# Attention in a one-core encoder layer: row maxima from the higher parts alone, as two 64-row products side by side

## The chip, the cores and the metric

One NeuronCore of a Trainium2 chip. The metric is the time of one launch of the whole layer in microseconds (us), median over runs. Engines: PE multiplies matrices (PEld is its loading of weights), DVE is the vector engine, ACT the scalar engine, POOL is GpSimd, SP issues transfers.

## What is computed

One encoder layer for two sequences, 512 and 1024 tokens, with shared weights. The change lies in its attention:

```python
q = apply_axial_rope(rms_norm(q.reshape(b, l, 16, 64), q_norm), cos, sin)
k = apply_axial_rope(rms_norm(k.reshape(b, l, 4, 64), k_norm), cos, sin)
s = jnp.einsum("bqgrd,bkgd->bgrqk", q_blk, k) * 64 ** -0.5
p = jax.nn.softmax(s, axis=-1)          # 16 query heads, 4 key heads
o = jnp.einsum("bgrqk,bkgd->bqgrd", p, v)
```

Before it come an RMS norm and the input projection, beside it a state-space branch and gates, after it the merge, an output projection and an MLP. The softmax is the same whatever number near the row's maximum is subtracted from the scores.

## The kernel before

The layer is one program in four parts: `project`, `gates_and_states`, `attention`, `tail`. Each engine's order of work is written out by hand, with semaphores between engines. A float32 value is held as a higher and a lower part (type fp32r), and a product is made as hi x hi + hi x lo + lo x hi.

Attention runs from about 633 to 1081 us of the span. A *unit* is one query head and one block of 512 queries: 16 units for the short sequence (A), 32 for the long one (B). A unit goes over the tiles of 128 keys, 4 in A and 8 in B; one tile is a *step*. There are 64 + 256 = 320 steps. In each step PE issues:

- the scores of the tile, transposed (keys by queries), two products (L1954, L1955): `k1` holds the higher part of the keys twice, in partitions 0 to 63 and 64 to 127, `q1` the higher and the lower part of the queries; `k2` holds the lower part of the keys in rows 0 to 63 and ones in row 64, `q2` the higher part of the queries and, in row 64, the negated maxima. So the second product has 65 rows, and the scores come out with the maximum subtracted.
- one product for the maxima of the unit *two units ahead* (`max_part`, L1923): 128 queries as the weights against 512 keys, 128 rows, so (hi + lo) queries x hi keys. In A one such product makes a bank of which DVE takes the maximum (L1831, 128x512); in B two products fill two banks and DVE reduces both at once (128x1024), so every second step. There are 56 + 256 = 312 of these products: 14 units of A with 4 and 32 of B with 8, the first two of B during the last two units of A, two in a step. Units 0 and 1 have theirs in `first_max` (L1521), ahead of attention.
- three products for the values of the step three steps back (`output`, L1905 with 128 columns of weights, L1906 with 64, L1908 with 128); the last waits for the lower part of the probabilities.

ACT takes the exponential of each score bank (L1789) and casts it to the higher part on odd steps (L1794); DVE casts on even steps (L1874), makes one lower part in four (L1864), and the maxima; POOL makes the other three lower parts (L1743). SP loads the queries of a unit into `q1` and `q2` (`load_q`, L189 to L191) when its last scores are done, and places the maxima in `q2` (`place_max` for A, L202; `place_max_parts` for B, L197). In A the queries of a maximum are every fourth one, so its weights are read with a stride of four elements; in B they are contiguous. Lines L163 to L209 are the class `Middle` with the places; POOL sets the row of ones at L1307, at the end of `gates_and_states`, after PE is done with the block of activations that lies there. PE turns and splits the values into banks of the maxima in the first iteration (L183, `V_TURN`), and waits for the split at the first steps of heads 2 and 3.

Of the kernel before, what the change touches and what calls it, by code (L numbers as in the profile page):

```python
# [27 lines left out]
P = 128  # L28
D_MODEL = 1024
D_FF = 4096  # L30
HEAD = 64
NQ, NKV = 16, 4
LEN_A, LEN_B = 512, 1024
TOK = LEN_A + LEN_B
BLK = 512
# [14 lines left out]
def f32(ap):  # L50

    return ap.bitcast(F32)
# [73 lines left out]
class Middle:  # L126
# [39 lines left out]
                         ).then_inc(landed, 16)  # L166

    def load_low_keys(self, sp, roped, n, tok, h0, h1):
        sp.dma_start(f32(self.k2[0:HEAD, h0:h1, tok]),
                     roped[1, NQ + h0:NQ + h1, :, tok].rearrange("h d n -> d h n")).then_inc(self.k_in[n], 16)  # L170

    def load_v(self, sp, proj, n, tok):
# [13 lines left out]
    def load_q(self, sp, roped, kv, head, blk):  # L186
        tok = bass.ds(blk * BLK, BLK)
        hi, lo = roped[0][head][:, tok], roped[1][head][:, tok]
        sp.dma_start(f32(self.q1[kv][0:HEAD]), hi).then_inc(self.q_in[kv], 16)  # L189
        sp.dma_start(f32(self.q1[kv][HEAD:P]), lo).then_inc(self.q_in[kv], 16)  # L190
        sp.dma_start(f32(self.q2[kv][0:HEAD]), hi).then_inc(self.q_in[kv], 16)  # L191

    def place_max_parts(self, sp, u, s):

        for j in range(BLK // P):
            sp.wait_ge(self.max_found, 4 * u + (2 + j + 1))
            sp.dma_start(f32(self.q2[s][HEAD:HEAD + 1, j * P:(j + 1) * P]),  # L197
                         f32(self.nmax[s][:, j:j + 1])).then_inc(self.nmax_in[s], 16)

    def place_max(self, sp, u, s):  # L200
        sp.wait_ge(self.max_found, 4 * u + (2 + BLK // P))
        sp.dma_start(f32(self.q2[s][HEAD:HEAD + 1]).rearrange("o (p j) -> o p j", p=P),  # L202
                     f32(self.nmax[s][:])).then_inc(self.nmax_in[s], 16)

    def max_query(self, kv, j, near=False):

        if near:
            return self.q1[kv][:, j * P:(j + 1) * P]
        return self.q1[kv].rearrange("d (p j) -> d j p", p=P)[:, j]  # L209


class Ahead:
# [773 lines left out]
def gates_and_states(nc, block, st, sh, mid, ps, w_in, proj, mix, roped, done):  # L986
# [12 lines left out]
    with ExitStack() as ctx:  # L999
# [82 lines left out]
        def all_batches(eng, batch):  # L1082

            batch(Batch(None, 0), True, False)
            with eng.Fori(0, BATCHES // 2 - 1) as i:
                batch(Batch(i, 1), False, False)
                batch(Batch(i, 2), False, False)
            batch(Batch(None, BATCHES - 1), False, True)
# [5 lines left out]
        def _(sp):  # L1094
# [71 lines left out]
                store_gate(5)  # L1166

            all_batches(sp, batch)
            mid.place_max(sp, 0, 0)
            mid.load_q(sp, roped, 3, 12, 0)  # L1170
            mid.place_max(sp, 1, 1)
# [72 lines left out]
        def _(pool):  # L1244
# [58 lines left out]
            pool.wait_ge(whi_ready, 2)  # L1303
            pool.tensor_tensor(w_lo[1][:], w_raw[1][:], f32(w_hi[1][:]), ALU.subtract).then_inc(wlo_ready, 1)
            all_batches(pool, batch)
            pool.wait_ge(summed, BATCHES * GB - 1)
            pool.memset(f32(mid.k2[HEAD:HEAD + 1]), 1.0).then_inc(mid.ones_set, 1)  # L1307

            pool.wait_ge(evicted, BATCHES * GB + 3)
            pool.wait_ge(mid.ones_set, 1)  # L1310

        @block.vector
        def _(dve):
# [227 lines left out]
def attention(nc, block, st, mid, fore, ps, proj, roped, mix_y, mix, mix_t, w_tail):  # L1541
# [7 lines left out]
    with ExitStack() as ctx:  # L1549
# [361 lines left out]
        @block.tensor  # L1911
        def _(pe):
            pe.sem_inc(pv_done, QKP)
            def max_part(sq, u, s, kt):

                per = sq.n // 4
                j, half = divmod(kt, per)
                if half == 0:

                    pe.wait_ge(max_found, 4 * u + (j - 1 if sq is A else j + 1))  # L1920
                bank = MX_BANK + (j if sq is A else 2 * (j % 2) + half)
                key0 = (sq.kt0 + 4 * half) * P
                mm = pe.matmul(ps[:, bank], mid.max_query(s, j, sq is B),  # L1923
                               k1[:, s, key0:key0 + BLK], start=True, stop=True)
                if half == per - 1:
                    mm.then_inc(max_mm, 1)

            for n, sq in enumerate(SEQS):
                pe.wait_ge(k_in[n], (16, 32 + 16 * NKV)[n])
                pe.wait_ge(ones_set, (1, 2 + B.n)[n])  # L1930

                def iteration(it, last):
                    for kv in range(NKV):
# [11 lines left out]
                        for kt in range(sq.n):  # L1945
# [3 lines left out]
                            if sq is A and isinstance(it, int) and it == 0 and kv == 0 and kt < 2:  # L1949
# [2 lines left out]
                            out = ps[:, ST_BANK + kt % 2]  # L1952
                            keys = slice(tile * P, (tile + 1) * P)
                            pe.matmul(out, k1[:, kv, keys], q1[kv][:], start=True, stop=False)  # L1954
                            pe.matmul(out, k2[0:HEAD + 1, kv, keys], q2[kv][0:HEAD + 1], start=False,  # L1955
                                      stop=True).then_inc(scored, 1)
                            if sq is A and isinstance(it, int) and it == 0:
                                if kv == 0 and kt == LAG:

                                    pe.wait_ge(v2_ready, 1)  # L1960
                                    pe.wait_ge(ones_set, 2)
                                if kv == 1 and kt == LAG:

                                    pe.wait_ge(v2_ready, 2)
                                if kv >= 2 and kt < 2:

                                    pe.wait_ge(v2_ready, 2 * kv - 1 + kt)
                            if sq is A and isinstance(it, int) and it == 0 and kv == 0 and kt == 0:

                                pe.wait_ge(mid.y_ready, GROUPS // BATCH + 1)  # L1970
                            if sq_ahead:
                                for part in range(sq_ahead.n // sq.n):
                                    max_part(sq_ahead, ahead, s_ahead, kt * (sq_ahead.n // sq.n) + part)
                            i = v_part(V_TURN, sq, it, kv, kt)
                            if i is not None:
                                pe.wait_ge(k_in[1], 32)
# [1067 lines left out]
```

## Time and profile before

| | |
|---|---|
| median of 3 runs | 2490.22 us (2488.33 to 2495.74) |
| span of the profiled execution | 2487.5 us |
| the profiled execution's own time | one of the above; which one is not told |
| PE / PEld busy | 2467.0 / 2192.8 us |
| DVE / ACT / POOL busy | 1690.4 / 1122.7 / 1081.6 us |
| granted TensorE clock | 1.000 |

The span runs from the first to the last instruction. The busy time of PE comes from modelled ends: a product's row is longer than the distance to the next product's start. The distance between starts is what a product takes in a dense stream. The start of a PEld row is the start of a weight load.

### The profile page before, as it was taken

What the parts mean: (1) busy time and instruction counts of PE and PEld (TensorE: products, weight loads), DVE (VectorE), ACT (ScalarE), POOL (GpSimd) and SP (SyncE); (2) the same over time, 40 slices, a digit from 0 to 9 for tenths busy, and PEclk for the clock granted to TensorE, in tenths of its full rate; (3) what the DMA queues carried; (4) which work ended last, traced back from release to release, by engine and by line L of the source; (5) the groups of instructions that cost most, each with busy time, mean ns of one, the idle gap of its engine ahead of it and who ended that gap; (6) DMA issues with size and microseconds to landing.
All of it is one profiled execution on the core that took longest, in us unless ns stands there. A gap on an engine that the chain in (4) does not pass through costs nothing.

```text
span 2487.5 us, 37690 instructions
## 1 busy us (share of the span) xinstructions
PE 2467.0 (99%) x12320; PEld 2192.8 (88%) x12320; DVE 1690.4 (68%) x2352; ACT 1122.7 (45%) x1902; POOL 1081.6 (43%) x906
## 2 busy tenths in 40 slices
PE   8999999999999999999999999999999999999999
PEld 6888888888777777778888889999999999999999
DVE  7986588988888888886666786444446854444442
ACT  7554122121777777763444344333334343333341
POOL 0004765654667766754444423333333343333332
PEclk9999999999999999999999999999999999999999
DMA  5445233232653121244656643222222432222221
GB/s 186 173 155 183 83 94 93 78 94 82 157 124 84 45 66 44 45 137 145 200 206 197 215 170 129 68 69 69 68 68 81 140 136 69 68 69 69 68 69 68
DMA packets 160253, 271.29 MB, mean 109 GB/s; under 512 B 47216, under 2 KB 63088, under 8 KB 159984
## 3 DMA queue, kind: packets, MB, share of 16 engines
q1 hardware_dynamic: 159824, 269.19, 34.4%
q8 instruction: 82, 1.34, 0.2%
q14 instruction: 59, 0.48, 0.1%
q10 hardware_dynamic: 288, 0.27, 0.0%
HBM read 200.08 MB, written 59.24 MB: 104 GB/s over the span
## 4 chain that ended last, share of the span: by engine, by line
PE 96%; DVE 2%; issue 1%; POOL 1%; DMA 1%; ACT 0%; ACTq 0%; SPq 0%; DVEq 0%; POOLq 0%
PE banks L63 16%; PE banks L65 16%; PE banks L64 16%; PE banks L2907 6%; PE banks L2909 6%; PE banks L2910 6%; PE p_acc L63 3%; PE p_acc L64 3%; PE p_acc L65 3%; PE banks L1955 3%; PE banks L1954 3%; PE banks L1908 3%; PE banks L1923 3%; PE banks L1906 3%; PE banks L1905 3%; PE banks L1493 1%
## 5 line engine op out<-in xcount | busy, mean ns | idle before, releaser
L63 PE MATMUL banks<-block,t_whi 128*128 128x384 f32 (+1 forms) x1088 | 386.5, 355 | 0.8 <-DVE t_x L2752 0.5
L65 PE MATMUL banks<-block,t_wlo 128*128 128x384 f32 (+1 forms) x1088 | 385.9, 355 | 0.0
L1743 POOL TENSOR_TENSOR a_plo<-a_p,a_phi 128x512 fp32r<-128x512 f32 x236 | 305.4, 1307 | 142.9 <-DVE a_phi L1874 135.9
L2689 DVE TENSOR_TENSOR f_x<-banks,f_x 128x384 f32<-128x384 f32 x256 | 142.6, 557 | 291.1 <-PE banks L65 285.7
L64 PE MATMUL banks<-block,t_whi 128*128 128x384 f32 (+1 forms) x928 | 331.9, 358 | 0.0
L2907 PE MATMUL banks<-block,t_whi 128*128 128x384 f32 x800 | 268.0, 335 | 2.1 <-DVE block L2820 0.8
L2910 PE MATMUL banks<-block,t_wlo 128*128 128x384 f32 x800 | 267.3, 334 | 0.0
L2427 POOL TENSOR_TENSOR t_wlo<-t_wraw,t_whi 128x1024 fp32r<-128x1024 f32 x67 | 164.2, 2451 | 219.2 <-ACT t_whi L2448 219.2
L2909 PE MATMUL banks<-block,t_whi 128*128 128x384 f32 x768 | 256.6, 334 | 0.0
L2432 POOL TENSOR_TENSOR t_wlo<-a_quotient,t_whi 128x512 fp32r<-128x512 f32 x96 | 142.1, 1480 | 220.0 <-ACT t_whi L2463 220.0
L1789 ACT ACTIVATE a_p<-banks 128x512 f32<-128x512 f32 x320 | 190.7, 596 | 95.9 <-PE banks L1955 86.9
L63 PEld LDWEIGHTS banks<-block,t_whi 128*128 128x128 f32 x1088 | 204.3, 188 | 17.8 <-issue 2.0
L65 PEld LDWEIGHTS banks<-block,t_wlo 128*128 128x128 f32 x1088 | 204.2, 188 | 15.1
L2432 POOL TENSOR_TENSOR t_wlo<-f_s,t_whi 128x512 fp32r<-128x512 f32 x64 | 84.3, 1317 | 268.6 <-ACT t_whi L2463 268.6
L2432 POOL TENSOR_TENSOR t_wlo<-t_wraw,t_whi 128x512 fp32r<-128x512 f32 x96 | 130.9, 1364 | 158.0 <-ACT t_whi L2463 157.9
L1831 DVE TENSOR_REDUCE stage<-banks 128x1 fp32r<-128x1024 f32 (+1 forms) x184 | 191.9, 1049 | 2.6 <-PE banks L1923 1.9
L64 PEld LDWEIGHTS banks<-block,t_whi 128*128 128x128 f32 x928 | 174.3, 188 | 15.4 <-issue 0.5
L2448 ACT ACTIVATE t_whi<-t_wraw 128x1024 fp32r<-128x1024 f32 x71 | 75.3, 1061 | 210.2 <-PE banks L65 204.9
L63 PE MATMUL p_acc<-block,w_hi 128*128 128x512 f32 x384 | 152.0, 396 | 8.7 <-DVE block L785 8.7
L2463 ACT ACTIVATE t_whi<-f_s 128x512 fp32r<-128x512 f32 x128 | 80.5, 630 | 170.6 <-PE banks L65 138.8
L2907 PEld LDWEIGHTS banks<-block,t_whi 128*128 128x128 f32 x800 | 150.2, 188 | 3.4 <-issue 2.4
L2463 ACT ACTIVATE t_whi<-a_quotient 128x512 fp32r<-128x512 f32 x112 | 70.7, 631 | 181.8 <-PE banks L65 161.9
(329 smaller groups left out, 6343.8 us busy)
## 6 DMA issues: line engine op xcount, KB each, us to landing
t_wraw<-w_tail_t SPq DMA_DIRECT2D x136, 512.0 KB, 3.8
a_quotient<-w_tail_t SPq DMA_DIRECT2D x64, 512.0 KB, 3.8
block<-roped_scratch SPq DMA_DIRECT2D x146, 128.0 KB, 2.7
w_raw<-w_in_t SPq DMA_DIRECT2D x31, 512.0 KB, 4.0
proj_scratch<-s_gate SPq DMA_DIRECT2D x48, 256.0 KB, 2.0
t_graw<-proj_scratch SPq DMA_DIRECT2D x24, 512.0 KB, 3.9
p_sw<-p_qn SPq DMA_DIRECT2D x60, 128.0 KB, 2.1
roped_scratch<-p_r_hi SPq DMA_DIRECT2D x30, 256.0 KB, 2.2
```

Source lines behind the costliest of these rows:

```text
L63: pe.matmul(out, whi, xhi, start=start, stop=False)
L64: pe.matmul(out, whi, xlo, start=False, stop=False)
L65: return pe.matmul(out, wlo, xhi, start=False, stop=stop)
L1743: pool.tensor_tensor(p_lo[s][:], p32[s][:], f32(p_hi[s][:]), ALU.subtract).then_inc(plo_pool, 1)
L1789: act.activation(p32[kt % QKP][:], ps[:, ST_BANK + kt % 2], ACT.Exp, scale=HEAD ** -0.5).then_inc(exp_done, 1)
L1831: dve.tensor_reduce(nmax[s][:, j:j + 1], src, AX.X if sq is A else AX.XY, ALU.max, negate=True).then_inc(max_found, 1)
L2427: pool.tensor_tensor(w_lo[j % 2][:], w_raw[j % 2][:], f32(w_hi[j % 2][:]), ALU.subtract).then_inc(wlo_ready, 1)
L2432: pool.tensor_tensor(ring_lo[t % 4], source(t), f32(ring_hi[t % 4]), ALU.subtract).then_inc(lo_pool.sem, 1)
L2463: act.activation(ring_hi[t % 4], source(t), ACT.Copy).then_inc(f_hi_ready, 1)
L2907: pe.matmul(out, ring_hi[s][:, k], x_hi, start=fresh and k == 0, stop=False, skip_group_check=True)
L2909: pe.matmul(out, ring_hi[s][:, k], x_lo, start=False, stop=False, skip_group_check=True)
L2910: mm = pe.matmul(out, ring_lo[s][:, k], x_hi, start=False, stop=last, skip_group_check=True)
```

## The change

The maxima are taken from the products of the higher parts alone (64 rows). Two such products, the first with rows 0 to 63 of `q1` and `k1`, the second with rows 64 to 127 of `q2` and `k1`, are issued one behind the other (`max_pair`): in A for two banks at steps 0 and 2 of a unit, at the seam for the two halves of one maximum in each step, in B for the two halves at every even step. For this the halves of `k2` and `q2` change places: lower keys and higher queries lie in rows 64 to 127, the ones in rows 0 to 63 of `k2`, the maxima in row 0 of `q2`, zeros in rows 1 to 63. The second score product has 128 rows. POOL clears four places of 64x512 before it sets the ones (now 64 rows), `ones_set` counts four more, SP waits for the four before the first placing, and PE waits for both value splits at step 0 of heads 2 and 3.

```diff
--- before.py
+++ after.py
@@ -166,7 +166,7 @@
                          ).then_inc(landed, 16)
 
     def load_low_keys(self, sp, roped, n, tok, h0, h1):
-        sp.dma_start(f32(self.k2[0:HEAD, h0:h1, tok]),
+        sp.dma_start(f32(self.k2[HEAD:P, h0:h1, tok]),
                      roped[1, NQ + h0:NQ + h1, :, tok].rearrange("h d n -> d h n")).then_inc(self.k_in[n], 16)
 
     def load_v(self, sp, proj, n, tok):
@@ -188,25 +188,26 @@
         hi, lo = roped[0][head][:, tok], roped[1][head][:, tok]
         sp.dma_start(f32(self.q1[kv][0:HEAD]), hi).then_inc(self.q_in[kv], 16)
         sp.dma_start(f32(self.q1[kv][HEAD:P]), lo).then_inc(self.q_in[kv], 16)
-        sp.dma_start(f32(self.q2[kv][0:HEAD]), hi).then_inc(self.q_in[kv], 16)
+        sp.dma_start(f32(self.q2[kv][HEAD:P]), hi).then_inc(self.q_in[kv], 16)
 
     def place_max_parts(self, sp, u, s):
 
         for j in range(BLK // P):
             sp.wait_ge(self.max_found, 4 * u + (2 + j + 1))
-            sp.dma_start(f32(self.q2[s][HEAD:HEAD + 1, j * P:(j + 1) * P]),
+            sp.dma_start(f32(self.q2[s][0:1, j * P:(j + 1) * P]),
                          f32(self.nmax[s][:, j:j + 1])).then_inc(self.nmax_in[s], 16)
 
     def place_max(self, sp, u, s):
         sp.wait_ge(self.max_found, 4 * u + (2 + BLK // P))
-        sp.dma_start(f32(self.q2[s][HEAD:HEAD + 1]).rearrange("o (p j) -> o p j", p=P),
+        sp.dma_start(f32(self.q2[s][0:1]).rearrange("o (p j) -> o p j", p=P),
                      f32(self.nmax[s][:])).then_inc(self.nmax_in[s], 16)
 
-    def max_query(self, kv, j, near=False):
-
+    def max_query(self, kv, j, near=False, rows=slice(0, P)):
+
+        queries = self.q2[kv] if rows.start else self.q1[kv]
         if near:
-            return self.q1[kv][:, j * P:(j + 1) * P]
-        return self.q1[kv].rearrange("d (p j) -> d j p", p=P)[:, j]
+            return queries[rows, j * P:(j + 1) * P]
+        return queries[rows].rearrange("d (p j) -> d j p", p=P)[:, j]
 
 
 class Ahead:
@@ -1166,6 +1167,7 @@
                 store_gate(5)
 
             all_batches(sp, batch)
+            sp.wait_ge(mid.ones_set, NKV)
             mid.place_max(sp, 0, 0)
             mid.load_q(sp, roped, 3, 12, 0)
             mid.place_max(sp, 1, 1)
@@ -1303,11 +1305,13 @@
             pool.wait_ge(whi_ready, 2)
             pool.tensor_tensor(w_lo[1][:], w_raw[1][:], f32(w_hi[1][:]), ALU.subtract).then_inc(wlo_ready, 1)
             all_batches(pool, batch)
-            pool.wait_ge(summed, BATCHES * GB - 1)
-            pool.memset(f32(mid.k2[HEAD:HEAD + 1]), 1.0).then_inc(mid.ones_set, 1)
+            for kv in range(NKV):
+                pool.wait_ge(summed, BATCHES * GB - 2 + kv // 2)
+                pool.memset(f32(mid.q2[kv][0:HEAD]), 0.0).then_inc(mid.ones_set, 1)
+            pool.memset(f32(mid.k2[0:HEAD]), 1.0).then_inc(mid.ones_set, 1)
 
             pool.wait_ge(evicted, BATCHES * GB + 3)
-            pool.wait_ge(mid.ones_set, 1)
+            pool.wait_ge(mid.ones_set, NKV + 1)
 
         @block.vector
         def _(dve):
@@ -1911,23 +1915,25 @@
         @block.tensor
         def _(pe):
             pe.sem_inc(pv_done, QKP)
-            def max_part(sq, u, s, kt):
-
-                per = sq.n // 4
-                j, half = divmod(kt, per)
-                if half == 0:
-
-                    pe.wait_ge(max_found, 4 * u + (j - 1 if sq is A else j + 1))
-                bank = MX_BANK + (j if sq is A else 2 * (j % 2) + half)
-                key0 = (sq.kt0 + 4 * half) * P
-                mm = pe.matmul(ps[:, bank], mid.max_query(s, j, sq is B),
-                               k1[:, s, key0:key0 + BLK], start=True, stop=True)
-                if half == per - 1:
-                    mm.then_inc(max_mm, 1)
+            def max_pair(sq, u, s, kt):
+
+                for i, rows in enumerate((slice(0, HEAD), slice(HEAD, P))):
+                    j, half = (kt + i, 0) if sq is A else (kt // 2, i)
+                    if sq is A:
+                        pe.wait_ge(max_found, 4 * u + (j - 1))
+                    elif half == 0:
+
+                        pe.wait_ge(max_found, 4 * u + (j + 1))
+                    bank = MX_BANK + (j if sq is A else 2 * (j % 2) + half)
+                    key0 = (sq.kt0 + 4 * half) * P
+                    mm = pe.matmul(ps[:, bank], mid.max_query(s, j, sq is B, rows),
+                                   k1[rows, s, key0:key0 + BLK], start=True, stop=True)
+                    if sq is A or half:
+                        mm.then_inc(max_mm, 1)
 
             for n, sq in enumerate(SEQS):
                 pe.wait_ge(k_in[n], (16, 32 + 16 * NKV)[n])
-                pe.wait_ge(ones_set, (1, 2 + B.n)[n])
+                pe.wait_ge(ones_set, NKV + (1, 2 + B.n)[n])
 
                 def iteration(it, last):
                     for kv in range(NKV):
@@ -1952,25 +1958,27 @@
                             out = ps[:, ST_BANK + kt % 2]
                             keys = slice(tile * P, (tile + 1) * P)
                             pe.matmul(out, k1[:, kv, keys], q1[kv][:], start=True, stop=False)
-                            pe.matmul(out, k2[0:HEAD + 1, kv, keys], q2[kv][0:HEAD + 1], start=False,
+                            pe.matmul(out, k2[:, kv, keys], q2[kv][:], start=False,
                                       stop=True).then_inc(scored, 1)
                             if sq is A and isinstance(it, int) and it == 0:
                                 if kv == 0 and kt == LAG:
 
                                     pe.wait_ge(v2_ready, 1)
-                                    pe.wait_ge(ones_set, 2)
+                                    pe.wait_ge(ones_set, NKV + 2)
                                 if kv == 1 and kt == LAG:
 
                                     pe.wait_ge(v2_ready, 2)
-                                if kv >= 2 and kt < 2:
-
-                                    pe.wait_ge(v2_ready, 2 * kv - 1 + kt)
+                                if kv >= 2 and kt == 0:
+
+                                    pe.wait_ge(v2_ready, 2 * kv)
                             if sq is A and isinstance(it, int) and it == 0 and kv == 0 and kt == 0:
 
                                 pe.wait_ge(mid.y_ready, GROUPS // BATCH + 1)
                             if sq_ahead:
-                                for part in range(sq_ahead.n // sq.n):
-                                    max_part(sq_ahead, ahead, s_ahead, kt * (sq_ahead.n // sq.n) + part)
+                                if sq_ahead is not sq:
+                                    max_pair(sq_ahead, ahead, s_ahead, 2 * kt)
+                                elif kt % 2 == 0:
+                                    max_pair(sq_ahead, ahead, s_ahead, kt)
                             i = v_part(V_TURN, sq, it, kv, kt)
                             if i is not None:
                                 pe.wait_ge(k_in[1], 32)
```

## Rows read from the trace of the kernel before

**Rows 1.** The page: its head and the busy time of each engine.

```profile
span 2487.5 us, 37690 instructions
PE 2467.0 (99%) x12320; PEld 2192.8 (88%) x12320; DVE 1690.4 (68%) x2352; ACT 1122.7 (45%) x1902; POOL 1081.6 (43%) x906
```

**Rows 2.** Stretches; busy us (count) of PE, PEld, DVE, ACT, POOL; clock, DMA, GB/s.

```profile
640.00:730.00 90.00, 88.62 (x383) 69.75 (x383) 79.71 (x125) 71.98 (x124) 61.37 (x55) 1.00 0.56 138
730.00:1060.00 330.00, 330.00 (x1429) 256.17 (x1429) 276.12 (x330) 250.52 (x423) 232.01 (x182) 1.00 0.23 55
1060.00:1077.00 17.00, 17.00 (x73) 12.36 (x72) 15.15 (x18) 15.41 (x28) 11.35 (x8) 1.00 0.09 16
```

**Rows 3.** The chain of waits from 730 to 1060 us, by line.

```profile
by line: PE banks L1955 17.0%; PE banks L1954 16.7%; PE banks L1906 16.5%; PE banks L1908 16.5%; PE banks L1923 16.4%; PE banks L1905 16.3%; DVE a_plo L1864 0.2%; DVE stage L1831 0.2%; issue 0.2%; DVE a_phi L1874 0.1%
```

**Rows 4.** Groups of PE, 730 to 1060 us: count | busy us, mean ns | idle.

```profile
L1955 PE MATMUL banks<-block 65*128 65x512 f32 x238 | 95.4, 401 | 0.0
L1954 PE MATMUL banks<-block 128*128 128x512 f32 x238 | 94.5, 397 | 0.0
L1923 PE MATMUL banks<-block 128*128 128x512 f32 x239 | 93.0, 389 | 0.0
```

**Rows 5.** Timeline of one step: start us, us, engine, line.

```profile
861.09 0.40 PE L1954 MATMUL banks<-block 128*128 128x512 f32 x1
...
861.32 0.40 PE L1955 MATMUL banks<-block 65*128 65x512 f32 x1
861.32 0.19 PEld L1923 LDWEIGHTS banks<-block 128*128 128x128 f32 x1
861.56 0.39 PE L1923 MATMUL banks<-block 128*128 128x512 f32 x1
...
861.79 0.39 PE L1905 MATMUL banks<-a_phi,a_v 128*128 128x512 f32 x1
...
862.01 0.39 PE L1906 MATMUL banks<-a_phi,a_v 128*64 128x512 f32 x1
...
862.24 0.39 PE L1908 MATMUL banks<-a_plo,a_v 128*128 128x512 f32 x1
...
862.47 0.40 PE L1954 MATMUL banks<-block 128*128 128x512 f32 x1
```

**Rows 6.** Line 1923 (ns least/median/most), and timelines near 641 and 728 us.

```profile
L1923 PEld LDWEIGHTS banks<-block x312: 186/191/311, 633.6 to 1059.6; 128*128 128x128 f32 x156
L1923 PE MATMUL banks<-block x312: 389/389/499, 633.8 to 1059.9; 128*128 128x512 f32 x156
...
640.74 0.31 PEld L1923 LDWEIGHTS banks<-block 128*128 128x128 f32 x1
...
728.33 0.19 PEld L1923 LDWEIGHTS banks<-block 128*128 128x128 f32 x1 [0.43 <-DVE stage L1831]
728.34 0.50 PE L1923 MATMUL banks<-block 128*128 128x512 f32 x1
...
728.67 0.39 PE L1905 MATMUL banks<-a_phi,a_va 128*128 128x512 f32 x1
```

**Rows 7.** DVE's reductions, 730 to 1060 us; waits of 640 to 730, 1060 to 1077.

```profile
L1831 DVE TENSOR_REDUCE stage<-banks 128x1 fp32r<-128x1024 f32 x119 | 144.4, 1213 | 2.6 <-PE banks L1923 1.9
...
PEld banks L1923 <- DVE stage L1831: 2.3, 5, 0.6
...
POOL a_plo L1743 <- DVE a_phi L1874: 6.6, 7, 1.4
PEld banks L1908 <- POOL a_plo L1743: 1.4, 4, 0.5
```

**Rows 8.** Timeline of POOL, and the chain of waits, before attention.

```profile
618.57 5.24 POOL L1307 MEMSET block<- 1x6144 f32 x1 [25.76 <-PE banks L65]
...
625.95 7.12 DMA block<-stage
633.27 0.47 PE banks L1954
```

## The prediction

> **What bounds the kernel now.** I read the page first: the product engine is busy 99% of the span, the vector engine 68%, GpSimd 43% [rows 1]. Then the stretches: the change touches only attention, about 633 to 1081 us, so what it is worth is read there. From 730 to 1060 us the sequence of 1024 tokens is swept and PE is busy 330.00 of 330 us; DVE is busy 276.12, ACT 250.52, POOL 232.01, at a granted clock of 1.00 [rows 2]. The chain of waits says the same from the other side: over that stretch six lines of PE hold 16 to 17% each and nothing else holds over 0.2% [rows 3]. So there a product less is time less, if nothing new is put beside it. From 640 to 730 us, the sequence of 512, PE is busy 88.62 of 90 and DVE 79.71 [rows 2]: still PE, with DVE close behind.
>
> The timeline of one step shows the unit of account. A step is six products, L1954 to L1954 from 861.09 to 862.47, that is 1.38 us or 0.23 for each [rows 5]. One of the six is the maximum's (L1923). The row of a product says 0.39 us, but its successor starts 0.23 later: 0.23 is the price of a product in a dense stream, and the other 0.16 is its modelled tail, hidden under the next one. The weights of a product are loaded at the start of the product before it (the load of L1923 at 861.32 beside L1955), so loads cost nothing now.
>
> **The products that go.** L1923 issues 312 products [rows 6]: 14 units of the short sequence of 4, and 32 of the long one of 8. They stay 312, but become 156 pairs of 64 rows, each pair on two halves of the array. Of the pairs, 28 are in the sweep of the short sequence, 8 at the seam (the last two units of the short sweep, working ahead for the long one), 120 in the long sweep. The work per product is the same 512 columns, so the gain is only what runs side by side: at best one slot of 0.23 per pair.
>
> What a pair costs has no row: no product of this kernel has 64 rows. I bound it by parts.
> - *Second load.* The weights of the second product need not be hidden, since the load ahead of it belongs to the first. The price of an exposed load does have a row: at 728.33 the load of L1923 came late, and the next product started at 728.67, 0.34 later in place of 0.23 [rows 6]. So 0.11 us. The bounds are 0 (both loads fit under the product before the pair) and 0.11. I take 0.11, for the trace always starts a load when the product before its own starts, and never two in one slot [rows 5].
> - *Changing the form of the array*, twice per pair. The nearest rows are other changes of form: 128 to 64 output columns and back (L1905 to L1906 to L1908) takes 0.22 and 0.23, and in and out of the product of 65 rows (L1955) takes 0.23 and 0.24 [rows 5]. So 0.01 per change is what they show. The far bound is a product that must have left the array before the next enters: its tail of 0.16 (0.39 less 0.23), and with the load waiting as well 0.27. No reason in the trace excludes it, since a change of 64 rows is another thing than one of columns. I take 0.01, by the nearest row.
>
> So a pair is 0.23 + 0.11 + 0.02 = 0.36 against 0.46: 0.10 saved. In the long sweep 120 x 0.10 = 12.0 us. In the short sweep the weights are read with a stride of four (the load of 0.31 us against 0.19 [rows 6]), so an exposed second load is 0.12 dearer, 0.23 in all, and the 28 pairs save nothing. At the seam DVE's long reductions are what is late (loads of L1923 waited 2.3 us for them, the longest 0.6 [rows 7]): 0 for the 8 pairs.
>
> On a page of the Trainium skill there is a rule against this change. "TensorEngine Tiling (Array Packing)", Key Properties, says that changing the tiling mode drains the engine. By it the small price of 0.01 is wrong and the far bound right; what that makes of the time is the slow rival below. The columns' rows do not show such a drain, but they bear on rows of the array only by analogy.
>
> **The second score product** goes from 65 rows to 128, the added ones zeros. A product costs its 512 columns, not its rows: 401 ns at 65 rows, 397 and 389 at 128 [rows 4]. If anything it gains: behind the 65-row product the next starts 0.24 later, not 0.23 [rows 5]. At most 320 x 0.01 = 3.2 us, at least 0; I take 1.6.
>
> **What moves on the queues.** SP issues the same transfers with other destinations; its one new wait, for the zeros, stands ahead of the first placing of maxima at 625.95 [rows 8]. POOL now clears four places of 64x512 before it sets the ones. The old setting, one row of 6144, took 5.24 us from 618.57 [rows 8], or 0.44 for 512. Two of the four clears come one gate tile earlier, so the ones start 0.9 later and end at about 624.7, before the transfer that attention waits for (625.95 to 633.07 [rows 8]). The four zeros are there by 619.5, so SP does not wait. Cost 0, covered by 8 us of that transfer; without the cover it would be 0.9, once.
>
> **The added wait.** In the first sweep PE waits at step 0 of heads 2 and 3 for the low half of the values that it formerly awaited at step 1. PE queues its output products behind it, and ACT then waits for scores. At most one step, 1.4 us, twice, at least 0; I take 1.5 together.
>
> **The other engines.** The maxima for two steps come in one, which makes the even steps 1.50 and the odd ones 1.15. A step without a maximum is already there: from 1060 to 1077 PE holds 73 products in 17 us, 0.23 each, with 1.4 us of waits for POOL [rows 2, 7]. In the long sweep, DVE's 276 us would be 87% of 318 us. A reduction takes 1213 ns, one per two steps [rows 7], and its banks come back two steps before they are needed, as now. I cost this at 0; what is late next is POOL's low part behind DVE's cast.
>
> **Sum:** -12.0 - 1.6 + 1.5 = -12.1 us. Of the execution profiled that is a span of 2487.5 - 12.1 = 2475.4; the time of this execution is not told apart among the three given, and their median, 2490.22, lies 2.7 above the span. I put the forecast on the median: 2478.
>
> **Rivals.**
> 1. *Everything side by side.* The two loads fit under the product before (two of 0.11 into 0.23), and the changes are free. Then 0.23 per pair: 120 x 0.23 = 27.6, still nothing for the strided pairs (two loads of 0.23 don't fit under one product), 3.2 of the 65 rows, 1.5 for the wait: -29, to 2461; with half of the gain for the strided pairs and no wait it would be 2456. For it: the loads' rates allow it. Against: never seen here, and DVE would be at 91% and begin to hold PE up. By itself: the skill's page "TensorE: Matmul & The Clock Gate", Part 3, has products on different row groups starting about 4 ns apart and four of them 3.07 times as fast, which speaks for this rival; no run here shows it yet.
> 2. *The array drains at each change.* The place is the product before the pair and the one behind it; with a price c per change, break-even is where 0.34 + 2c = 0.46, at c = 0.06. With the tail, c = 0.16, a pair takes 0.66: +0.20, x 120 = 24; the strided pairs (0.23 + 0.23 + 0.32) +0.32 x 28 = 9; together +33, to 2523. With the load exposed too, c = 0.27: +0.42 x 120 and +0.54 x 28, +65, to 2555. For it: the far bound, and nothing in the trace excludes it. Against: four changes of form per step that cost 0.01 at most.
> 3. *The halves don't run together*, so that the change doesn't do what it says: 64 rows at 0.23 each, loads hidden, changes free. Then only the small terms are left: 0, 2490. For it: a product of 65 rows costs the same as one of 128, and matmuls in this trace always start one after the other.
>
> **How the numbers follow.** The measurement tells 0.3%, some 7.5 us, from no change. Chances: forecast 0.34, rival 1 0.13, rival 2 0.38 (0.12 of it with the load exposed), rival 3 or a price near break-even 0.15. Faster by over 0.3%: 0.34 + 0.13 = 0.47; the same 0.16, with a little of rival 2; slower 0.37. Because both signs are likely, the forecast's own range is 2468 to 2484; the range to hold the time 8 times in 10 reaches from rival 1's lower bound, 2456, to rival 2's lower price, 2524, and leaves out the dearer drain.
>
> **What would show it.** In the timeline of the long sweep: the second of a pair starting 0.11 (forecast), about 0 (rival 1) or 0.23 (rival 3) behind the first, and the product behind the pair 0.23 after the second. Rival 2 shows as gaps: over 0.3 from L1955 to the pair, or from the pair to the values' product. The stretch of 120 pairs should shrink from 330 to 318 us, all six other groups unchanged. I am wrong if PE gets idle time in the long sweep, if waits for POOL's low part or DVE's reduction grow past 3 us, or if attention starts later than now.

## The result, and the profile after

The changed kernel takes 2518.56 us (median of 4 runs, 2517.70 to 2519.42) beside 2492.02 for the kernel before: ratio 1.0109, 95% interval 1.0092 to 1.0126. It is slower by 27 us where 12 us less were forecast. Its span is 2516.9 us. The runs of the kernel before fall into two groups, near 2489 and near 2495 us, so that its median moves by up to 2.5 us from one comparison to the next (2489.54 to 2492.02); the traces are of single runs.

The head of the page answers to [rows 1]. PE is still busy 99% of the span, so a look at the busy time says nothing: what has grown is PE's own time.

```profile
span 2516.9 us, 37692 instructions
PE 2495.6 (99%) x12320; PEld 2152.3 (86%) x12320; DVE 1671.0 (66%) x2352; ACT 1113.9 (44%) x1902; POOL 1082.6 (43%) x910
```

The stretches answer to [rows 2], in the same columns. From 730 to 1060 us PE is busy throughout, as before, but it gets through 1347 records where it had 1429. DVE has fallen from 276 to 249 us, ACT from 251 to 227: they wait for PE. In the short sweep the clock's mean is 0.99.

```profile
640.00:730.00 90.00, 88.07 (x354) 56.85 (x353) 66.48 (x116) 65.39 (x113) 56.06 (x50) 0.99 0.52 127
730.00:1060.00 330.00, 330.00 (x1347) 210.28 (x1346) 248.81 (x311) 226.90 (x396) 219.60 (x172) 1.00 0.23 57
```

The chain over the long sweep, which answers to [rows 3], names PE alone again, with one share out of line: 22.5% for the first product of the values, L1909, which stands right behind the pair.

```profile
by line: PE banks L1909 22.5%; PE banks L1960 15.7%; PE banks L1912 15.7%; PE banks L1910 15.6%; PE banks L1961 15.6%; PE banks L1929 15.0%
```

The timeline shows why. The first step holds a pair, the second none (L1960 and L1961 are the scores, L1929 the pair, L1909, L1910, L1912 the values; start us, us, engine, line):

```profile
899.67 0.40 PE L1960 MATMUL banks<-block 128*128 128x512 f32 x1
899.91 0.39 PE L1961 MATMUL banks<-block 128*128 128x512 f32 x1
...
900.23 0.19 PEld L1929 LDWEIGHTS banks<-block 64*128 64x128 f32 x2 [0.36 <-issue]
900.23 0.50 PE L1929 MATMUL banks<-block 64*128 64x512 f32 x2
...
900.66 0.19 PEld L1909 LDWEIGHTS banks<-a_phi,a_v 128*128 128x128 f32 x1 [0.25 <-ACT a_phi L1798]
900.66 0.50 PE L1909 MATMUL banks<-a_phi,a_v 128*128 128x512 f32 x1
...
901.00 0.40 PE L1910 MATMUL banks<-a_phi,a_v 128*64 128x512 f32 x1
...
901.46 0.39 PE L1960 MATMUL banks<-block 128*128 128x512 f32 x1
...
901.69 0.40 PE L1961 MATMUL banks<-block 128*128 128x512 f32 x1
...
901.93 0.39 PE L1909 MATMUL banks<-a_phi,a_v 128*128 128x512 f32 x1
...
902.15 0.39 PE L1910 MATMUL banks<-a_phi,a_v 128*64 128x512 f32 x1
```

Three things differ from [rows 5]. The load of the pair's weights starts 0.32 us behind L1961 (899.91 to 900.23), not at its start: it has waited for the slot of L1961, 0.23, and 0.09 more. The load of L1909 starts 0.43 behind that of the pair, again not beside a running product. And L1910 follows L1909 by 0.34, the 0.11 of an exposed load. From L1961 to L1910 that is 1.09 us; in the step without a pair it is 0.46 (901.69 to 902.15). So a pair takes 0.63 us, where its two products took 0.46 before: +0.17, and 120 of them make 20 us. The pairs of the long sweep are alike: from L1961 to L1910 it is 1.08 to 1.10 us in each of them from 740 us on. The timeline merges the two products of the pair into one row; their own starts in the trace are 900.230 and 900.233, and the starts of their weight loads 900.228 and 900.232, so both start together, 3 or 4 ns apart. The cast of ACT that the row at 900.66 names as releaser is not what L1909 waits for: it casts the step before the pair's (899.90 to 900.53), and the values are three steps behind; x3 and x4 move the load by 0.23 with the group's length.

That can be checked over the whole sweep, by the first and the last product of the values with the long sequence's lower parts. Before:

```profile
L1908 PE MATMUL banks<-a_plo,a_v x256: 387/392/503, 733.3 to 1088.6; 128*128 128x512 f32 x128
```

and after:

```profile
L1912 PE MATMUL banks<-a_plo,a_v x256: 387/393/505, 743.5 to 1118.8; 128*128 128x512 f32 x128
```

355.3 us has become 375.3. The other 9.4 us of the span's growth (2516.9 - 2487.5 = 29.4) lie ahead of the long sweep: it starts 10.2 us later, with the start of attention at the same 633.3 us; what follows the sweep is 0.8 us shorter. Of the 10.2 us, 2.6 have been lost by the first such product of the short sweep (639.3 in place of 636.7), in steps that ran in part at half clock (see x8). POOL's clears end where I put them (three rows of its timeline; 624.73 is ahead of the transfer that attention waits for):

```profile
613.12 0.98 POOL L1310 MEMSET block<- 64x512 f32 x2 [20.33 <-PE banks L65]
618.56 0.99 POOL L1310 MEMSET block<- 64x512 f32 x2 [4.46 <-PE banks L65]
619.50 5.23 POOL L1311 MEMSET block<- 64x6144 f32 x1
```

### The profile page after: what moved, and what is told of

It is laid out like the page before. It is cut to its first block, busy times and chain, and to the rows that moved or that the text cites. A ratio compares the mean times of both kernels' runs of the same rounds, so it can differ in the third digit from the quotient of the medians.

```text
span 2516.9 us, 37692 instructions
## 1 busy us (share of the span) xinstructions
PE 2495.6 (99%) x12320; PEld 2152.3 (86%) x12320; DVE 1671.0 (66%) x2352; ACT 1113.9 (44%) x1902; POOL 1082.6 (43%) x910
## 4 chain that ended last, share of the span: by engine, by line
PE 96%; DVE 2%; DMA 1%; issue 1%; ACT 0%; POOL 0%; SPq 0%; DVEq 0%; POOLq 0%; ACTq 0%
PE banks L63 16%; PE banks L65 16%; PE banks L64 16%; PE banks L2915 6%; PE banks L2918 6%; PE banks L2917 6%; PE banks L1909 4%; PE p_acc L63 3%; PE p_acc L64 3%; PE p_acc L65 3%; PE banks L1960 3%; PE banks L1912 3%; PE banks L1961 3%; PE banks L1929 3%; PE banks L1910 3%; PE banks L1497 1%
## 5 line engine op out<-in xcount | busy, mean ns | idle before, releaser
L1878 DVE CAST a_phi<-a_p 128x512 fp32r<-128x512 f32 x160 | 91.9, 574 | 101.2 <-ACT a_p L1793 95.6
```

## The experiments

Theory D, from the timeline above: a change between 128 and 64 rows holds the next weight load back until the array is empty (0.09 us), and the load is then exposed (0.11 us), so 0.20 at either end of a pair; the pair itself runs side by side. Its rivals are the schedule (S), halves that don't overlap, and the clock. Where I say *sweep*, I mean the time between the first and the last product L1912 (L1908 before) of the long or the short sequence, as in the two rows above; each is from one execution.

### x1: the changed kernel with 128 rows

```diff
                 for i, rows in enumerate((slice(0, HEAD), slice(HEAD, P))):
...
+                    if full:
+                        rows = slice(0, P)
                     mm = pe.matmul(ps[:, bank], mid.max_query(s, j, sq is B, rows),
```

(`full` is true in both calls)

> Keeps all of the change but the 64 rows: the two products of a pair are issued one behind the other in the same steps, each with 128 rows (higher and lower parts of the queries again). Theory D (a change between 128 and 64 rows makes the next weight load wait until the array is empty, about 0.09 us, and then exposes the load, 0.11 us, at both ends of a pair): no change of form is left, so the long sweep takes 355 us as before and the time is 2488 to 2494 us. Rival S (the new schedule costs the time: products of two steps bunched in one, the earlier wait for the value splits, 128 rows in the second score product): the time stays near the changed kernel's 2518.

2495.80 us beside 2489.95, ratio 1.0022 (1.0012 to 1.0032). So of the 28.6 us from 2489.95 to the changed kernel 22.8 belong to the 64 rows, and 5.8 (0.22% by the ratio) to all the rest of the change: more than theory D allowed, much less than rival S wants. The long sweep took 357.9 us:

```profile
L1912 PE MATMUL banks<-a_plo,a_v x256: 387/396/505, 737.7 to 1095.6; 128*128 128x512 f32 x128
```

Another part is the earlier wait for the value splits, in the short sweep (the waits of 640 to 735 us: us in total, times, longest). The weight loads wait for 2.8 us in two waits, and PE itself is idle for 1.9 of them, where I had put 1.5. Neither the kernel before nor x5, which has the old waits back, has such a row.

```profile
PEld banks L1931 <- DVE a_v L1846: 2.8, 2, 1.4
...
PE banks L1931 <- DVE a_v L1846: 1.9, 2, 1.0
```

### x2: pairs in the long sweep alone

```diff
-                                    max_pair(sq_ahead, ahead, s_ahead, kt)
+                                    max_pair(sq_ahead, ahead, s_ahead, kt, sq is A)
```

(the last argument, `full`, takes 128 rows; the same at the seam)

> 64-row pairs only in the sweep of the long sequence (120 pairs); the 36 pairs of the short sweep have 128 rows. Theory D: 120 times 0.167 us = +20 over the kernel before, about 2510; the half clock at 635 to 641 us and the 10 us that the short sweep has lost are gone. Rival C (the half clock comes from bunching or from the waits, not from the 64 rows): the clock still falls at 635 us and the time is 2513 to 2520.

2511.57 us, 1.0090 (1.0075 to 1.0105). As theory D wants, the long sweep is that of the changed kernel to the tenth, 375.3 us, and the clock is 1.00 from 633 to 642 us:

```profile
L1912 PE MATMUL banks<-a_plo,a_v x256: 388/394/506, 736.1 to 1111.4; 128*128 128x512 f32 x128
```

Against x1, the same program but for the 120 pairs, that is 15.8 us in the medians and 17.4 in the sweep, 0.13 to 0.15 a pair; against the kernel before it is 0.17, since x1's own sweep is 2.6 us longer than that kernel's. Of these, 1.6 are in x5 too, whose products are not bunched.

### x3 and x4: is the pair side by side?

```diff
-                for i, rows in enumerate((slice(0, HEAD), slice(HEAD, P))):
+                for n in range(4 if full else 2):
+                    i, rows = n % 2, (slice(0, HEAD), slice(HEAD, P))[n % 2]
```

(`full` is true in the long sweep, here and in x4; here the maxima are announced behind the fourth product)

> The changed kernel, but each of the 120 pairs of the long sweep is issued twice in a row (the same four operands, the second pair writes over the first), so one group of four products of 64 rows between two changes of form. Side by side: a further pair costs one slot, 0.22 to 0.23 us, so 120 times that, +27 over the changed kernel, about 2545. Rival (the halves run one after the other, the pair's cost being in them and not in the changes): +0.46 each, +55, about 2573.

2546.48 us in its one run, 27.9 over the changed kernel, 0.23 for each further pair. The group of four between two changes (the rows of L1962, of the group, of L1909):

```profile
902.00 0.39 PE L1962 MATMUL banks<-block 128*128 128x512 f32 x1
902.32 0.73 PE L1930 MATMUL banks<-block 64*128 64x512 f32 x4
902.98 0.49 PE L1909 MATMUL banks<-a_phi,a_v 128*128 128x512 f32 x1
```

0.66 from the group to L1909, where a single pair has 0.43: a second pair costs 0.23, one slot for two products. The single starts behind these rows show both changes: the first pair starts 0.32 behind L1962, the second pair 0.34 behind the first (902.316 to 902.651), L1909 0.32 behind the second, and L1910 0.34 behind L1909. So a change costs the same 0.09 and 0.11 on the way in and on the way out, and between the pairs the load of the second is hidden.

```diff
+                    if full:
+                        rows = slice(0, HEAD)
                     mm = pe.matmul(ps[:, bank], mid.max_query(s, j, sq is B, rows),
```

> The changed kernel, but in the long sweep both products of a pair use rows 0 to 63 (same values computed), so they cannot run side by side. Theory D with the pair side by side: the second product costs a slot, +0.23 times 120 = +27, about 2545. Rival (the two halves already run one after the other): unchanged, 2518.

2544.78 us, in one run too. The same two products on one half:

```profile
901.34 0.39 PE L1963 MATMUL banks<-block 128*128 128x512 f32 x1
901.66 0.73 PE L1931 MATMUL banks<-block 64*128 64x512 f32 x2
902.32 0.51 PE L1909 MATMUL banks<-a_phi,a_v 128*128 128x512 f32 x1
```

0.66 again, so 0.23 more than on two halves. Together the two runs show that the halves do run side by side, and that a slot of 0.23 is all that there is to gain. The two changes cost what is left: 0.63 less 0.23, 0.40. One change is 0.20 us.

### x5: the places alone

The kernel before with the halves exchanged, the zeros, and 128 rows in the second score product; single products at their old steps, old waits.

```diff
-                            pe.matmul(out, k2[0:HEAD + 1, kv, keys], q2[kv][0:HEAD + 1], start=False,
+                            pe.matmul(out, k2[:, kv, keys], q2[kv][:], start=False,
```

> The kernel before with the new places alone: halves of the second keys and queries exchanged, zeros, second score product of 128 rows; the maxima are single products of 128 rows at their old steps, and the old waits for the value splits are back. Theory: the places are free, 2487 to 2491 us, and the 5.5 us by which full_rows lay over the kernel before belong to its bunched products and its earlier wait. Rival: the places cost them (128 rows, zeros, transfers), 2494 to 2497.

2491.58 us, 0.9995 (0.9985 to 1.0005). The medians show no cost of the places, POOL's clears and the 63 rows of zeros, but a small one is not excluded: all of x5's runs are in one group, from 2489.79 to 2492.30, and the lower group of the kernel before, ten of its 18 runs beside it, has a median of 2488.9. The long sweep is 1.6 us longer than in the kernel before:

```profile
L1912 PE MATMUL banks<-a_plo,a_v x256: 387/396/502, 733.0 to 1089.9; 128*128 128x512 f32 x128
```

On average over the starts from 745 to 1055 us, the product behind the second score product does start 0.231 us after it in place of 0.240, as forecast. But other products start some ns later than before, and a step takes 1.393 us in place of 1.387. Why is open.

### x7 and x8: the short sweep

```diff
-                                    max_pair(sq_ahead, ahead, s_ahead, kt)
+                                    max_pair(sq_ahead, ahead, s_ahead, kt, sq is B)
```

(`full` takes 128 rows in the long sweep)

> 64-row pairs only in the short sweep and at its seam (36 pairs), full products in the long sweep. Theory: the half clock at 635 to 641 us is back, and the time is full_rows' 2496 plus about 6: 2500 to 2504. Rival (the loss of the short sweep in the changed kernel is bunching and waits, not the 64 rows): 2496.

2500.64 us, 1.0031 (1.0019 to 1.0042), and the clock fell as expected, to 0.50 from 634 to 637 us. It is 4.8 over x1, on average 0.13 for each of the 36 pairs. That is not what such a pair takes. A strided pair of the changed kernel:

```profile
702.38 0.40 PE L1961 MATMUL banks<-block 128*128 128x512 f32 x1
702.71 0.62 PE L1929 MATMUL banks<-block 64*128 64x512 f32 x2
703.26 0.50 PE L1909 MATMUL banks<-a_phi,a_va 128*128 128x512 f32 x1
703.60 0.39 PE L1910 MATMUL banks<-a_phi,a_va 128*64 128x512 f32 x1
```

From L1961 to L1910 that is 1.22 us, where the step without a pair has 0.46: 0.76 for a strided pair. It is 0.13 dearer than a contiguous one, because the load that is exposed behind the change is the longer, strided one (0.55 from the pair to L1909 in place of 0.43). The median of these stretches is 1.22 in x7 too, and 0.93 in x1, so a strided pair loses 0.29 there. For 28 pairs, and 0.17 for each of the 8 at the seam, that would be 9.5 us; the 4.8 are less because x1 waits for transfers and reductions in this sweep where x7 does not (PE is idle for them for 1.6 us in x1, for nothing in x7). The rest of the difference is not accounted for.

```diff
-                                    max_pair(sq_ahead, ahead, s_ahead, kt)
+                                    max_pair(sq_ahead, ahead, s_ahead, kt, sq is A and isinstance(it, int) and it == 0)
```

> The changed kernel with 128-row products in the first iteration of the short sweep (four units) alone. Theory (the sparse first steps with drained pairs let the clock fall): the granted clock stays at 1.00 from 633 to 650 us and the time falls by 3 to 5 us below the changed kernel, 2514 to 2516. Rival (the clock falls later instead, or its fall costs nothing): 2518.

2516.66 us, 1.0090 (1.0074 to 1.0105). It is 1.9 below the changed kernel, where 3 to 5 were expected, and the reason given for that fell: the clock halved all the same (stretches in the columns of [rows 2]; the clock is the third figure from the end):

```profile
633.00:634.00 1.00, 0.65 (x2) 0.58 (x3) 0.00 (x0) 0.00 (x0) 0.00 (x0) 0.71 1.00 291
634.00:635.00 1.00, 1.00 (x4) 0.81 (x3) 0.00 (x0) 0.48 (x1) 0.00 (x0) 0.50 1.02 406
...
637.00:638.00 1.00, 1.00 (x6) 0.78 (x5) 0.00 (x0) 1.00 (x3) 0.12 (x1) 1.00 0.00 0
```

In the changed kernel it stayed at 0.50 (1.2 GHz) for longer:

```profile
633.00:634.00 1.00, 0.67 (x4) 0.34 (x4) 0.00 (x0) 0.00 (x0) 0.00 (x0) 1.00 0.90 318
634.00:635.00 1.00, 1.00 (x4) 0.60 (x4) 0.30 (x1) 0.60 (x1) 0.00 (x0) 0.63 1.06 430
640.00:641.00 1.00, 1.00 (x4) 0.35 (x3) 1.00 (x2) 0.19 (x1) 0.99 (x1) 0.50 0.60 172
641.00:642.00 1.00, 1.00 (x5) 0.55 (x6) 0.69 (x2) 0.41 (x1) 1.00 (x2) 0.95 0.61 211
```

Kernel x6, below, has no pair before the long sweep, and there it fell too:

```profile
633.00:640.00 7.00, 6.20 (x20) 4.69 (x20) 2.94 (x6) 4.23 (x8) 1.29 (x1) 0.76 0.50 167
640.00:650.00 10.00, 9.95 (x49) 7.98 (x49) 10.00 (x16) 7.84 (x15) 8.62 (x8) 1.00 0.27 70
```

So the 64 rows are not needed to make it fall. In the profiles of the changed kernel, x3, x4, x6, x7, x8 and x9 it fell, 2.3 to 3.6 us after PE had gone idle at about 631 us, waiting for the first maxima; in six of them it was back after 3.4 us, in the changed kernel after 6.8. In those of the kernel before, x1, x2, x5, x10 and x11 it stayed at 1.00. The idle time does not tell them apart: PE stood idle for 2.07 to 2.84 us where it fell, and for 1.61 to 3.17 where it did not (2.59 in the kernel before, 2.66 in the changed one). The profiles are of one execution each, and the kernel before need not be free of it: ten of its 18 runs beside x5 have a mean clock of 0.999 and not 1.000, and so have all four of the changed kernel; where in the run the clock was lower is not recorded. Which executions it takes, and whether drained pairs make it last longer, is open.

### x6, x9, x10, x11: fewer changes of form

If a change costs 0.20 and a pair 0.23, two pairs between the same changes take 0.46 + 0.40 = 0.86 us, four single products 0.92. All four are built on x5, with pairs in the long sweep alone. In x6 DVE takes the maxima at the first and the second step of every four.

```diff
+                                if sq is B and kt % 4 == 0:
+                                    max_pair(B, ahead, s_ahead, kt)
+                                    max_pair(B, ahead, s_ahead, kt + 2)
```

> As the layout run, but in the long sweep the products of two pairs are issued in one go at every fourth step (four products of 64 rows between two changes of form), and the reductions of those maxima moved to the steps right behind them. Theory D: a group costs 2 x 0.23 + 0.40 = 0.86 us where four single products cost 0.92, so 60 x 0.06 = 3.6 us less than the layout run, about 2485. Rival (the larger bunch delays scores, and POOL and DVE with them): 2489 to 2495.

2509.60 us, 1.0060 (1.0046 to 1.0074), far above the 2485 of theory D and above the rival's 2489 to 2495 too. The loss was in DVE's order: its two reductions, one behind the other, made its casts and POOL's lower part late. The waits of 735 to 1090 us have a row for the load of the values' last product, where the kernel before has 2.0 us in 5 waits:

```profile
PEld banks L1915 <- POOL a_plo L1747: 35.8, 74, 1.6
```

x9 puts the reductions back at their old steps, the second and the fourth, and x10 at the second and third, where DVE's low part and a cast still come between them:

```diff
-                                if kt % 4 < 2:
-                                    find_max(ahead, it * 4 + (sq.u0 + kv + 2), (kv + 2) % 4, 2 * (kt // 4) + kt % 4)
+                                per = sq.n // 4
+                                if kt % per == per - 1:
+                                    find_max(ahead, it * 4 + (sq.u0 + kv + 2), (kv + 2) % 4, kt // per)
```

> As x6_quads, but DVE takes the maxima at its old steps, the second and the fourth of every four, in place of two in a row. Theory R (x6's loss is DVE's two reductions in a row, which make its cast and POOL's low part late, not the group of four products): the waits for POOL's low part, 35.8 us in x6, fall below 8 us. What is late next is the product behind the reduction of the fourth step: if it waits under 0.1 us a group, 2486 to 2490 us; if it waits for half a reduction, 60 x 0.6 = 36 us are lost instead. Rival (the bunch of four itself delays the scores, so the waits for POOL stay): 2505 or more.

> As x6_quads, but DVE takes the maxima at the second and third step of every four, behind its cast and its low part of the third step. Theory R: between x6's 2509 and the 2487 that the count of the products gives, since the two reductions still lie close together: 2487 to 2498. Rival (the bunch of four delays the scores): 2505 or more.

2498.96 us, 1.0025 (1.0015 to 1.0035), and 2498.80 us, 1.0028 (1.0017 to 1.0038), both above what was expected if nothing else came late. The waits for POOL are down to 1.5 and 2.0 us, what the kernel before has; what x9's expectation named as late next is late. In x9 products of the group (L1943) wait for the reduction of the banks that they write, 31 times for 10.3 us in all. The other row, called issue, is the load that the change holds back:

```profile
PEld banks L1943 <- issue: 21.4, 59, 0.4
...
PEld banks L1943 <- DVE stage L1835: 10.3, 31, 0.8
```

```profile
901.27 0.39 PE L1975 MATMUL banks<-block 128*128 128x512 f32 x1
...
901.59 0.18 PEld L1943 LDWEIGHTS banks<-block 64*128 64x128 f32 x2 [0.36 <-issue]
...
902.47 0.49 PE L1909 MATMUL banks<-a_phi,a_v 128*128 128x512 f32 x1
```

0.88 from the group's start to L1909 where 0.66 would do. This is the loss of x9: its long sweep is 363.5 us, 6.6 more than x5's, where the count gives 3.6 less. x11 gives the reduction time: PE issues the group at the end of its step.

```diff
-                                if sq is B and kt % 4 == 0:
-                                    max_pair(B, ahead, s_ahead, kt)
-                                    max_pair(B, ahead, s_ahead, kt + 2)
...
                                 output(pe, sq, unit - 1, (kv + 3) % 4, kt - LAG + sq.n, step - LAG,
                                        four(sq, it, kv, kt - LAG))
+                            if sq_ahead and sq is B and kt % 4 == 0:
+                                max_pair(B, ahead, s_ahead, kt)
+                                max_pair(B, ahead, s_ahead, kt + 2)
```

> As x9_quads_13, but PE issues the group of four at the end of its step, behind the three products for the values, 0.7 us later, so that DVE has taken the maximum of the banks before. Theory: the group takes 0.66 us again in place of 0.83, 60 x 0.17 = 10 us less than x9: 2487 to 2491, the kernel before within 0.2%. Rival (the scores of the next step now come 1 us later, and ACT, DVE and POOL with them): 2495 or more, with waits for scores or for POOL's low part.

2486.83 us (11 runs, 2486.10 to 2487.70) beside 2489.54, ratio 0.9984 (0.9975 to 0.9993). The group takes 0.66 to the next scores, and no wait is in it (L1943 is the group, L1974 and L1975 the scores):

```profile
899.64 0.73 PE L1943 MATMUL banks<-block 64*128 64x512 f32 x4
900.30 0.50 PE L1974 MATMUL banks<-block 128*128 128x512 f32 x1
900.64 0.40 PE L1975 MATMUL banks<-block 128*128 128x512 f32 x1
...
904.82 0.39 PE L1912 MATMUL banks<-a_plo,a_v 128*128 128x512 f32 x1
905.14 0.74 PE L1943 MATMUL banks<-block 64*128 64x512 f32 x4
```

This version beats both kernels: by 0.16% of the kernel before, and by 32 us the changed one. The gain over the kernel before is small but not the work of its upper group of runs: all 11 runs of x11 lie below all 15 of that kernel beside it (2487.83 at the least), and against their lower group, 2489.0, it is about 2 us. The long sweep is 352.7 us, where the kernel before has 355.3 and x5, on which it is built, 356.9:

```profile
L1912 PE MATMUL banks<-a_plo,a_v x256: 388/396/505, 733.0 to 1085.7; 128*128 128x512 f32 x128
```

Against x5 that is 4.2 us less; the count gives 60 x 0.06 = 3.6.

## Why the prediction was wrong

The sign was wrong. The measured time, 2518.56, lies in the range of 2456 to 2524, but far above the forecast's own 2468 to 2484. It was the cheaper form of rival 2 that happened, to which I gave 0.26 of its 0.38.

- **What bounds the kernel** was right: PE held the long sweep, and its product time is what the change moved.
- **The step that failed** is "Changing the form of the array", taken at 0.01 "by the nearest row". It measured 0.20 at either end of a pair, and 0.32 at the start of a strided one, whose exposed load is longer. The rows were near by name alone: from 128 to 64 columns and from 128 to 65 rows no load had ever been held back, which the same timeline could have told me, for in each of them the next load starts with the product (the two rows below, with [rows 5]). My far bounds, 0.16 for the tail and 0.27 with the load, stood on either side. The rule that I cited beside it, of the Trainium skill's "TensorEngine Tiling (Array Packing)", Key Properties, that a change of mode drains the array, agrees with the trace: at each change the load is held back by 0.09 us, and being exposed costs 0.11 more. That the array is empty at that moment is not shown: the ends of products are modelled, and L1961's row ends at 900.30, behind the load at 900.23.

```profile
861.79 0.13 PEld L1906 LDWEIGHTS banks<-a_phi,a_v 128*64 128x64 f32 x1
862.02 0.19 PEld L1908 LDWEIGHTS banks<-a_plo,a_v 128*128 128x128 f32 x1
```

- **The second load**, taken at 0.11, costs 0: both products start together, and x3 shows 0.23 for a further pair. That is as the Trainium skill's page "TensorE: Matmul & The Clock Gate", Part 3, has it, products on different row groups starting some 4 ns apart; in the trace it is 3 ns (900.230 and 900.233).
- Put together, the pair was forecast at 0.36 us and takes 0.63. Rival 2's 0.66 was near for a wrong reason: its c of 0.16 is too low, and the 0.11 of the second load is too much. Rival 3, halves one after the other, is refuted by x3 and x4; rival 1 was right of the pair and wrong of its ends. The break-even that I gave, c = 0.06, assumed the exposed load; it is 0.115 without it, and one change is beyond either.
- **The strided pairs** were forecast at 0.46 us, no gain and no loss, and take 0.76, which rival 2 put at 0.78; in the time x7 less x1 is 4.8 us, seam included. That the strided load is 0.12 dearer when exposed was right; but it is the first load that is exposed, not the second.
- **The second score product**, forecast at 1.6 less: no gain in the time (x5, 0.9995). The 0.01 per step is there in the trace, and lost again at the other products.
- **The added wait**, forecast at 1.5: PE is idle for 1.9. **Bunching** was costed at 0. Beside x5, x1 is 3.6 us longer in the short sweep (98.8 against 95.2) and 1.0 in the long one, so wait and bunching together are 4.6. For the argument of the odd and even steps I took a stretch with one reduction in it (1060 to 1077 us) as if it held for one with a reduction at every second step; x6 shows how little slack DVE's order has.
- **The moved places and queues**, forecast at 0, cost at most the 2 or 3 us by which x5 lies above the lower group of the kernel before; attention starts at the same 633.3 us.

By x1, x7 and the changed kernel the medians split so: 5.8 for all but the 64 rows, 4.8 for the 36 pairs, 17.9 for the 120. These runs stem from different comparisons, so each part is good to 2 or 3 us.

## What to carry to other kernels

Packing two 64-row products into one slot saves one slot per pair and costs two changes of form, 0.40 us against 0.23 here, so it pays only when at least two pairs stand between the same two changes. Where a price has no row of its own, ask what the near row shares with it (here: whether a load is held back), and not how alike they sound. And when products are regrouped, move the readers of their banks with them: the same group of four gave +0.60%, +0.25% and -0.16% by the order around it alone.

## What the runs showed of the hardware

- A change between products of 128 and of 64 rows costs 0.20 us, in either direction: the next weight load starts 0.32 us after the start of the last product in place of 0, and is exposed. Between 64-row products there is none, on two halves (x3) or on one (x4).
- Two 64-row products on two halves start 3 ns apart and take one slot, 0.23 us; on the same half they take two.
- After 1.6 to 3.2 us of idle time of PE ahead of attention the granted clock was at 0.50 in seven of 13 profiled executions, for 3.4 us or, in one, 6.8, and stayed at 1.00 in six.
